# The first pair's gates before the attention steps, and a query's rotation inside its gates, in the first mixer of a three-stage network

## The reference, cut to what matters

```
px = hx @ w_in                       # q: 16 heads of 64, k and v: 4 heads, z: gate, 1024 wide
q  = apply_axial_rope(rms_norm(q, q_g), cos, sin)     # x only; the context's q is normed, not rotated
s  = einsum('bqkgd,bskd->bkgqs', qi, k_all) * ATTN_SCALE     # x sees context and x: 768 keys
p  = softmax(s);  o = einsum('bkgqs,bskd->bqkgd', p, v_all)
yx = (o * silu(z)) @ w_out
# the same for the context's 256 queries, which see the 256 context keys alone
```

## Time and profile before

| | |
|---|---|
| median of three executions | 1726.72 us |
| the profiled execution | 1720.33 us, span 1718.6 us |
| granted TensorE clock, mean over the span | 0.958 |
| steps 0 to 47 of mixer A's attention | 101.39 us to about 512 us of the span |
| TensorE busy in the span | 1589.8 us, 93% |

### The profile page before, as it was taken

One profiled execution on the slowest core, in us unless ns is written; L12 is line 12 of the kernel. 1 busy time (PEld: TensorE's weight loads), 2 busy tenths in 40 slices (PEclk: granted clock), 3 DMA queues, 4 the chain that ended last, 5 costly groups with the idle time before them and its releaser, 6 DMA issues.

```text
span 1718.6 us, 25018 instructions
## 1 busy us (share of the span) xinstructions
PE 1589.8 (93%) x9858; PEld 1237.7 (72%) x9858; DVE 720.4 (42%) x1702; ACT 613.7 (36%) x1291; POOL 660.4 (38%) x652
## 2 busy tenths in 40 slices
PE   5998998888989799999998889999999898999997
PEld 4776766666768688888886768878887875655855
DVE  4344434434452524544445453524332363455033
ACT  4243344333453223333334342434322243333221
POOL 2433333333342434343334444345245243332252
PEclk8999989999999899999999889999999899999998
DMA  9121220110003222222220302122121221110221
GB/s 379 50 75 50 74 72 29 73 71 28 26 2 133 88 75 80 80 75 80 80 75 25 123 31 98 49 74 99 49 98 50 98 74 69 55 50 25 74 76 71
DMA packets 22148, 128.20 MB, mean 75 GB/s; under 512 B 2448, under 2 KB 2576, under 8 KB 8080
## 3 DMA queue, kind: packets, MB, share of 16 engines
q1 hardware_dynamic: 21888, 126.35, 20.2%
q10 hardware_dynamic: 144, 0.26, 0.1%
HBM read 124.50 MB, written 2.10 MB: 74 GB/s over the span
## 4 chain that ended last, share of the span: by engine, by line
PE 79%; DVE 9%; issue 4%; ACT 4%; POOL 2%; DMA 2%; SPq 0%; POOLq 0%; DVEq 0%; ACTq 0%
PE PS L1356 14%; PE PS L1358 13%; PE PS L1357 13%; PE PS L1436 7%; PE PS L1471 6%; PE PS L1446 6%; PE PS L1351 3%; PE PS L1601 3%; PE PS L1352 3%; PE PS L1353 3%; DVE sm L2031 2%; PE PS L1611 1%; POOL WL L2346 1%; PE PS L1369 1%; DMA XC<-in_xt 1%
## 5 line engine op out<-in xcount | busy, mean ns | idle before, releaser
L2346 POOL TENSOR_TENSOR WL<-W,WH 128x512 fp32r<-128x512 f32 x280 | 364.5, 1318 | 337.7 <-ACT WH L1631 337.7
L1356 PE MATMUL PS<-HX,WH 128*128 128x512 f32 x1008 | 417.5, 414 | 16.5 <-DVE LX L1952 11.9
L1357 PE MATMUL PS<-LX,WH 128*128 128x512 f32 x1008 | 398.3, 395 | 0.0
L1358 PE MATMUL PS<-HX,WL 128*128 128x512 f32 x1008 | 398.0, 395 | 0.0
L1356 PEld LDWEIGHTS PS<-HX,WH 128*128 128x128 f32 x1008 | 193.0, 191 | 65.8 <-issue 23.5
L1358 PEld LDWEIGHTS PS<-HX,WL 128*128 128x128 f32 x1008 | 192.2, 191 | 42.4
L1357 PEld LDWEIGHTS PS<-LX,WH 128*128 128x128 f32 x1008 | 193.0, 191 | 35.7 <-issue 1.9
L1631 ACT CAST WH<-W 128x512 fp32r<-128x512 f32 x296 | 172.0, 617 | 49.7 <-DMA W<-in_wu 42.3
L2031 DVE TENSOR_REDUCE sm<-PS 128x1 f32<-128x512 f32 (+4 forms) x224 | 150.1, 670 | 84.0 <-PE PS L1436 79.5
L1708 ACT ACTIVATE AR<-PS,sm 128x768 f32<-128x768 f32 (+4 forms) x160 | 115.5, 722 | 180.7 <-DVE sm L2036 101.1
L2402 POOL TENSOR_SCALAR AR<-AR,sm 128x768 f32<-128x768 f32 (+1 forms) x96 | 74.0, 771 | 230.5 <-DVE sm L2047 230.5
(11 more groups left out here) (268 smaller groups left out, 2480.7 us busy)
## 6 DMA issues: line engine op xcount, KB each, us to landing
W<-in_wu SPq DMA_DIRECT2D x98, 1024.0 KB, 4.8
AR<-in_wu SPq DMA_DIRECT2D x8, 1024.0 KB, 11.6
AR<-in_biasb SPq DMA_DIRECT2D x32, 256.0 KB, 2.6
XX<-in_xt SPq DMA_DIRECT2D x2, 1024.0 KB, 5.9
out<-XX SPq DMA_DIRECT2D x8, 256.0 KB, 2.2
XC<-in_xt SPq DMA_DIRECT2D x1, 1024.0 KB, 14.1
C<-in_cc SPq DMA_DIRECT2D x1, 770.5 KB, 8.4
CS<-in_cs SPq DMA_DIRECT2D x1, 512.0 KB, 9.9
```

The lines of the kernel that those rows point to most:

```text
L1356: e.matmul(o, wh, xh, start=(k == 0), stop=False)
L1357: e.matmul(o, wh, xl, start=False, stop=False)
L1358: t = e.matmul(o, wl, xh, start=False, stop=(k == 7))
L2346: e.tensor_tensor(WL[:, d, a:z], W[:, n % 2, a:z], WH[:, d, a:z].bitcast(F32), ALU.subtract).then_inc(*s_wl_pool.by(n, q))
```

## The change

The gates of pair 0 move out of the fill into the stage ahead of step 0: between the turning of query 0 and the last group of values. The fill starts with pair 1's query. In each pair the query's sums, turning and rotation all go into the 8 blocks of x's gates (after block 1, block 3 and block 6), the turning takes bank 7 instead of bank 6, and the context's gates follow behind the rotation. The second mod of a pair moves from x's gates to the context's gates and takes bank 6 instead of bank 7. Pair 7 is treated like the others. The order of the weight units follows, and the share of fill for each step is reckoned with the smaller amount.

```diff
--- before.py
+++ after.py
@@ -49,9 +49,9 @@
 def unit_order():
 
     m = [("mod", 0, i) for i in range(8, 12)] + [("mod", 1, i) for i in range(12)]
-    u = [("ak",), ("av",), ("aqz", 0), m[0]]
+    u = [("ak",), ("av",), ("aqz", 0)]
     for i in range(1, 8):
-        u += [("aqz", i)] + m[2 * i - 1:2 * i + 1 if i < 6 else 12]
+        u += [("aqz", i)] + (m[2 * i - 2:2 * i] if i < 7 else [])
     for i in range(4):
         u += [("aout", i), m[12 + i]]
     for a in range(4):
@@ -787,43 +787,31 @@
 
         units_, riding = iter(MA[:12]), [iter(())]
 
-        def ride_mm():
+        def ride_mm(pr=FC):
 
             for l, u in units_:
-                riding[0] = mod_units(l, (u,), FC)
+                riding[0] = mod_units(l, (u,), pr)
                 next(riding[0])
                 return
+
+        def ride_mm_x():
+            ride_mm(FX)
 
         def ride_tr():
             next(riding[0], None)
             riding[0] = iter(())
 
         def fill_a():
-            yield from gate_group(0, 0, FX, {3: ride_mm, 7: ride_tr})
-            yield PAUSE
-            yield from gate_group(0, 1, FC)
-            yield PAUSE
             for pair in range(1, 8):
                 yield from until(lambda: pair < 2 or pair - 2 in done_a)
                 yield from query_group(pair, 0, FX, {1: ride_mm, 5: ride_tr})
                 yield PAUSE
                 yield from query_group(pair, 1, FC)
                 yield PAUSE
-                if pair < 7:
-                    yield from gate_group(pair, 0, FX, {1: lambda: query_sums(pair, FC), 3: ride_mm, 7: ride_tr})
-                    yield PAUSE
-                    yield from gate_group(pair, 1, FC, {3: lambda: query_turn(pair, FX)})
-                    query_rope(pair)
-                    yield PAUSE
-            query_sums(7, FC)
-            yield PAUSE
-            query_turn(7, FX)
-            yield PAUSE
-            query_rope(7)
-            yield from gate_group(7, 0, FX)
-            yield PAUSE
-            yield from gate_group(7, 1, FC)
-            yield PAUSE
+                yield from gate_group(pair, 0, FX, {1: lambda: query_sums(pair, FC), 3: lambda: query_turn(pair, FC), 6: lambda: query_rope(pair)})
+                yield PAUSE
+                yield from gate_group(pair, 1, FC, {1: ride_mm_x, 6: ride_tr})
+                yield PAUSE
             yield from begin_out("aout", "o", parts_a, done_a, FA)
         values((0, 1))
         key_work[0]()
@@ -836,10 +824,12 @@
         query_sums(0, vr)
         values((4,))
         query_turn(0, vr)
+        run(gate_group(0, 0, vr))
         query_rope(0)
+        run(gate_group(0, 1, vr))
         values((5,))
         unv.done(s_proj, "av", 5)
-        attention("a", [s for pair in range(8) for s in steps_a(pair)], SA, TA, PbA, PTbA, OA, fill_a(), (8 * 15 * (T + LC) + 14 * T) / 100 + 7 * 3, posted_a)
+        attention("a", [s for pair in range(8) for s in steps_a(pair)], SA, TA, PbA, PTbA, OA, fill_a(), (8 * 14 * (T + LC) + 14 * T) / 100 + 5 * 3, posted_a)
         do("a_last_gate")
 
         residual = {}
```

## The result

The change made the kernel faster by more than forecast: 1703.67 us in the median of four runs (1701.25 to 1706.76) against 1726.08 us (1722.9 to 1727.49) for the kernel before on the same chip, a ratio of 0.9874 with a 95% interval of 0.985 to 0.9897. The profiled execution took 1702.07 us, its span is 1700.3 us. The forecast of 1716 and the lower end of its range, 1704, are both above the measured time, the lower end by 0.3 us.

The account below looks back on a forecast made before the run. TensorE, busy in 93% of the span, bounds the kernel, leaving its waits and clock to gain. Opening +4.8, starts -11.15, clock -4.5, pair 7 0 sum to -10.9: 1709.5 us profiled, 1716 on the median's scale; range 1704 to 1728.

Parts of the forecast that it names:

- The opening: Start to step 7: gates ahead of step 0, late split of pair 1's unit and its load; 4.8 us lost.
- The pairs' starts: Steps around the starts of pairs 2 to 6: fill lies in the waits there; 11.15 us won, ends 1.5 and 19.
- The new wait: Step before a pair's start, pairs 2 to 6: the mod's sums wait 1.3 us for x's gate on DVE.
- The clock: Steps 13, 19 and 31, at half clock behind pairs' starts: three quarters of 6.1 us recovered, 4.5 us won.
- Pair 7 and the end: Pair 7, to step 42: sums leave the query, turning and rotation come nearer; taken as 0, between -2 and +2 us.
- The scale: Whole kernel: 6.4 us added to 1709.5, as the profiled execution was that far under the median; 1715.9, said as 1716.
- the clock goes on falling: Rival, chance 0.20: starts are filled but the falls stay and step 0's is not hidden; -3.9 us, 1722.8.
- the rotation holds up x's gate: Rival, chance 0.10: late rotation on DVE delays x's gate, mod's sums stop TensorE at five starts; +7.2 us, 1733.9.
- everything at the starts goes: Rival, chance 0.12: all waits at pairs' starts (3.8 us each) and half clocks of steps 13, 19, 31 go; 1706.4.

Follow-up runs that it names:

- the first experiment: Kernel after with pair 0's gates put back into the fill of step 0, the rest of the change kept: 1690.62 us, ratio 0.9801 to the kernel before.
- the fourth to eighth: Kernel after: last values before pair 0's gates, 1692.55 us; mod later, 1698.9; gates in fill, sums later, 1682.15; that plus mod later, 1672.36; values-first, sums and mod later, 1675.79.
- the tenth: Fastest kernel (gates in fill, sums and mod later, 1672.36 us) with pair 7's sums, turning and rotation after blocks 1, 3 and 6 again: 1671.98 us.
- the second and third experiments: Kernel before with only pair 0's gates in the opening and new unit order, 1732.7 us; kernel after with pairs 1 to 6's rotation behind context's gates, 1730.21 us.

## Why the prediction was wrong

**The opening: right within 0.9 us, in part because errors cancel.** Forecast: step 0 8.5 later, steps 0 and 1 21.8 us, step 7 4.8 us later, with a wait of 5.3 us for POOL. Measured 7.5, 22.35, 5.7 and 5.4. Steps 2 to 6 took 37.45 us instead of 36.1, at a mean clock of 0.94. Step 0 took 14.4 instead of 12.2, as its matmuls ran at half clock behind the wait; step 1 gave most of it back (7.95) because its cast was still waiting for the load, as the prediction said the half clock would be hidden. Three rows of the kernel after, TensorE's wait, POOL's subtraction and, in step 1, ACT's cast behind the load:

```profile
115.86 0.76 PE L1346 MATMUL PS<-HX,WH 128*128 128x512 f32 x1 [5.44 <-POOL WL L2336]
...
114.44 4.96 POOL L2336 TENSOR_TENSOR WL<-W,WH 128x512 fp32r<-128x512 f32 x4 [0.50 <-ACT WH L1621]
...
126.82 0.62 ACT L1621 CAST WH<-W 128x512 fp32r<-128x512 f32 x1 [5.99 <-DMA W<-in_wu]
```

**The pairs' starts: mechanism right, 13.4 us instead of 11.15.** The new wait is there as worked out, 1.37 us instead of 1.3, for x's gate:

```profile
212.88 1.07 PE L1359 MATMUL PS<-W,sm 128*32 128x256 f32 x16 [1.37 <-DVE AR L2001]
```

Steps 10, 11 and 12 of a period at full clock take 7.21, 7.08 and 5.70 (forecast 7.6, 7.0 to 7.3, 5.7). The turning in place of a mod's sums made step 10 shorter by 0.35, not equal. That gives 1.5 over four pairs; the rest is pair 6, which won 1.9 instead of 1.1.

**The clock: the step that failed.** The term took three quarters of the 6.1 us lost in steps 13, 19 and 31, 4.5. Measured is 9.3 in the five periods and 1.1 more in step 37 (9.30 at 0.82 to 8.17 at 1.00, the same list), 10.4 in all, above even the term's upper end of 6.1 and some 3. Two errors make it. First, I took a quarter off for falls that would stay, and none stayed: behind a filled start no step fell below full clock, in none of the five of the kernel after and in none of the 39 of the first experiment and the fourth to eighth and the tenth. Behind unfilled starts 25 of 28 fell (five of six before, six of six in the second and third experiments). Second, I counted only the falls at the windows that I had read, and left out steps 16, 34 and 37; the first two lie behind the query's sums, a wait that stood in the earlier trace rows's view one row below the two that I used. That these two went may be chance, as said above.

The Trainium skill's "TensorE: Matmul & The Clock Gate", section "HAM oscillation — how this bites in real kernels", tells of a kernel in which waits for DMA of some 3 to 5 us throttle the array anew, each time. The wait of 5.44 us in step 0 agrees, with a clock of 0.76 in that step. The prediction read the Trainium skill too widely when it put every pair's start under this rule: the waits there are 1.62 and 2.21 us. What such shorter waits do, only the rows show, and they do it not every time: steps 22 and 28 of before and steps 16, 22, 28 and 34 of after kept full clock behind the same 0.93 us that stood ahead of step 10.

**Pair 7 and the end: 2.4 won instead of 0**, 1.1 of it step 37's clock.

**The scale.** I added 6.4 us because the profiled execution of before was so far under the median. For the kernel after that gap is 1.6 (1702.07 against 1703.67). Of the 12.3 us between forecast and result, 7.4 is the sum (-18.3 against -10.9) and 4.8 this step. In the sum, the clock's term was 4.8 too small without step 37, the starts' 2.3 and the end's 2.4; the opening lost 0.9 more, and the rest of the program 1.2.

**The rivals.** That the clock goes on falling is refuted by steps 13 to 31 at 1.00. That the rotation holds up x's gate is refuted: the waits at the mod's sums never exceed 1.4 us. The third, everything at the starts goes, came nearest in time (1706.4). Its half clocks went as it says; its waits did not, as 13.4 us were won instead of 19 and the new wait came, five times.

## What to carry to other kernels

When a kernel is bound by TensorE, go through all its repeated waits, the ones under 1 us too, and read the granted clock of the step behind each; price a wait as itself plus what the clock takes there. Moving a small dependent job two blocks later, behind work that is ready, won 18 us here (the mod's sums moved with it), most of what the whole change won. And when work is put ahead of a stage, ask first which unit's release it delays: one move of the last values won back 6.3 us up to step 7, where the opening had lost 5.7. One profiled execution doesn't tell how often the clock falls: the same kernel shows falls at some places and not at their like, so a gain in clock counts as a change's own only where the change altered the wait ahead of it.

## What was not expected of the hardware

A wait of 0.93 us ahead of twelve matmuls of two columns was followed by a stretch at a clock of 0.81 (step 10 of before, 9.21 us against 7.56 at full clock) in some pairs and not in others of one execution. Without the wait it never was: pairs 1 to 6 of the five kernels that list the sums later are thirty such places. And the price of the same wait at a pair's start, for the same list of work, was mostly 2.35 us in one kernel and 1.03 in another, whose lists differ only in where the query's sums and the mod's sums stand, half a period earlier.
